# The S5 convolution kernel in four column groups, and its Toeplitz rows through DRAM

## The reference

```python
def s5_layer(u, lam_re, lam_im, log_dt, b_re, b_im, c_re, c_im, d_skip):
    ...
    bu_re = jnp.einsum('blgh,gph->blgp', uf, bb_re)
    bu_im = jnp.einsum('blgh,gph->blgp', uf, bb_im)
    ...
    _, _, xr, xi = lax.associative_scan(combine, (a_re, a_im, bu_re, bu_im), axis=1)
    y = (jnp.einsum('blgp,ghp->blgh', xr, c_re.astype(f32))
         - jnp.einsum('blgp,ghp->blgh', xi, c_im.astype(f32))
         + d_skip.astype(f32) * uf)
```

## Time and profile before

| | |
|---|---|
| time, median of 3 runs (least to most) | 980.72 us (980.63 to 980.98) |
| the profiled execution: its time / its span | 982.18 us / 980.4 us |
| TensorE busy | 895.5 us (91%) |
| VectorE / ScalarE / GpSimd busy | 303.9 / 179.2 / 168.0 us |
| moved by DMA | 254.32 MB, 259 GB/s on average |
| mean granted TensorE clock | 0.987 of full speed |

### The profile page before, as it was taken

The page is one execution under the profiler, slowest core; times in us unless marked ns, Lnnn a source line. Parts: engine busy times, 40 slices in busy tenths (PEclk is TensorE's granted clock), DMA queues, the critical chain, the costliest instruction groups (busy, mean ns, idle before and its releaser), DMA issues.

```text
span 980.4 us, 14278 instructions
## 1 busy us (share of the span) xinstructions
PE 895.5 (91%) x4978; PEld 508.5 (52%) x4978; DVE 303.9 (31%) x810; ACT 179.2 (18%) x403; POOL 168.0 (17%) x264
## 2 busy tenths in 40 slices
PE   8999999999999999999978898889888988887884
PEld 3445876554444444445845555555555555554432
DVE  4990675770111111125651111111111111111125
ACT  1222148661000000101111111111111111111121
POOL 2010013440000000000002222222222222222212
PEclk9999999999999999999989999999999999999978
DMA  8342844028322222091589999999999999999963
GB/s 311 72 82 98 100 46 162 2 76 369 136 75 75 76 75 76 10 380 44 204 350 422 417 420 421 422 420 421 421 422 420 423 422 421 425 420 425 423 250 145
DMA packets 44266, 254.32 MB, mean 259 GB/s; under 512 B 15103, under 2 KB 15631, under 8 KB 27812
## 3 DMA queue, kind: packets, MB, share of 16 engines
q1 hardware_dynamic: 33702, 243.38, 62.8%
q0 software_dynamic: 10240, 9.64, 3.8%
q10 hardware_dynamic: 288, 0.81, 0.2%
HBM read 256.28 MB, written 21.04 MB: 283 GB/s over the span
## 4 chain that ended last, share of the span: by engine, by line
PE 77%; SPq 8%; DMA 4%; DVE 4%; issue 3%; ACT 1%; POOLq 0%; POOL 0%; DVEq 0%; ACTq 0%
PE ps L671 20%; PE ps L810 16%; PE ps L830 9%; PE ps L449 6%; PE ps L707 6%; DMA reg_bo<-experts 4%; SPq L348 4%; SPq L355 3%; PE ps L441 3%; PE ps L797 2%; PE ps L628 2%; PE ps L584 2%; PE ps L606 2%; PE ps L510 2%; PE ps L820 1%
## 5 line engine op out<-in xcount | busy, mean ns | idle before, releaser
L810 PE MATMUL ps<-arena,reg_a 128*64 128x256 f32 x1024 | 117.8, 381 | 4.9 <-DMA arena<-experts 3.0
L1568 DVE TENSOR_TENSOR small<-reg_u,ps 128x128 f32<-128x128 f32 x62 | 17.9, 288 | 333.7 <-ACT reg_u L1067 333.7
L671 PE MATMUL ps<-xT,arena 128*128 128x512 f32 x256 | 111.2, 592 | 0.0
L810 PEld LDWEIGHTS ps<-arena,reg_a 128*64 128x64 f32 x1024 | 86.8, 138 | 43.7 <-issue 21.8
L1711 POOL DMA_INDIRECT ye_scratch<-reg_bo,reg_u x62 | 62.7, 1011 | 223.9 <-ACT reg_bo L1074 221.5
L671 PEld LDWEIGHTS ps<-xT,arena 128*128 128x128 f32 x256 | 48.6, 190 | 61.2 <-issue 61.2
L830 PE MATMUL ps<-arena,small 128*64 128x512 f32 x256 | 63.7, 616 | 13.9 <-issue 9.9
L1074 ACT COPY reg_bo<-ps 128x512 f32<-128x512 f32 x62 | 36.3, 585 | 208.8 <-PE ps L830 205.5
L671 PE MATMUL ps<-reg_u,arena 128*128 128x512 f32 x128 | 57.5, 592 | 0.0
L707 PE MATMUL ps<-reg_a,reg_bo 128*128 128x512 f32 x128 | 55.8, 593 | 0.0
L449 PE MATMUL ps<-xT,reg_bo 128*128 128x512 f32 x128 | 55.7, 594 | 0.0
(11 more groups left out here) (287 smaller groups left out, 1189.3 us busy)
## 6 DMA issues: line engine op xcount, KB each, us to landing
arena<-experts SPq DMA_DIRECT2D x32, 2048.0 KB
arena<-experts SPq DMA_DIRECT2D x32, 1024.0 KB
reg_bo<-experts SPq DMA_DIRECT2D x8, 2048.0 KB
reg_a<-experts SPq DMA_DIRECT2D x8, 2048.0 KB
arena<-mid_w SPq DMA_DIRECT2D x8, 1792.0 KB, 7.4
xT<-experts SPq DMA_DIRECT2D x7, 2048.0 KB
x<-experts SPq DMA_DIRECT2D x7, 2048.0 KB
reg_bo<-experts SPq DMA_DIRECT2D x8, 1024.0 KB
```

What stands on the lines that cost most here:

```text
L671: m = pe.matmul(ps[bank][:, :], w[:, (o + c) * P:(o + c + 1) * P], rhs[:, c, :], start=(c == 0), stop=(c == nk - 1))
L810: m = pe.matmul(ps[2 + c % 2][64 * h:64 * h + 64, 0:DE], xgT[:, x, BLK * (c % 2):BLK * (c % 2 + 1)], gates[k][:, x * 512 + h * DE:x * 512 ...
```

## The change

The products that make the convolution kernel are placed otherwise. Pair g = 4b + q now goes to the 32 rows of column group q and to 128 columns at block b of a single bank; the loops run b, then real and imaginary part, then q, so that consecutive products go to different column groups. One copy of 128 rows by 512 columns takes the whole bank to `kst`. The constants of the skip term (`s5d`, `eyeh`) are laid out for 128 rows, and VectorE's product of the two no longer waits for the copies.

The matrix `kst` is then written to DRAM (`kst_scratch`, 256 KB) in one transfer, counted by the new semaphore `s_kd`. The Toeplitz rows are read from there: eight transfers, one for each k, with 512 pieces each, of the same lengths as before. Five are issued by SP after the bias transfers, three by ScalarE ahead of the v copies; both wait for `s_kd`. TensorE waits once for the copy ahead of the v projection where it waited for one bank each time, and for 8 Toeplitz transfers instead of 16.

```diff
@@ -95,6 +95,7 @@
         SKEW, SKEW_C = 16, 8
         shift_dram = nc.dram_tensor("shift_scratch", (SKEW, HEADS, WB), F32, kind="Internal").ap()
         shift_c_dram = nc.dram_tensor("shift_c_scratch", (SKEW_C, HEADS, 2 * L), F32, kind="Internal").ap()
+        kst_dram = nc.dram_tensor("kst_scratch", (P, 4 * P), F32, kind="Internal").ap()
         x1_dram = nc.dram_tensor("x1_scratch", (L, D), F32, kind="Internal").ap()
         ye_dram = nc.dram_tensor("ye_scratch", (2 * 2 * L, D // 2), F32, kind="Internal").ap()
 
@@ -107,8 +108,8 @@
         b2row = sm.take(HD)
         post = sm.take(2 * SP2).rearrange("p (i m) -> p i m", i=2)
         posb = sm.take(2 * 2 * SP2).rearrange("p (i g m) -> p i g m", i=2, g=2)
-        s5d = sm.take(GP, 32)
-        eyeh = sm.take(SH, 32)
+        s5d = sm.take(4)
+        eyeh = sm.take(SH)
         rtbl = sm.take(HEADS, 33)
 
 
@@ -151,7 +152,7 @@
         apow = s5r.take(2 * GP * 9).rearrange("p (i g j) -> p i g j", i=2, g=GP)
         sp = [s5r.take(GP) for _ in range(40)]
         w1t = x1[:, :].rearrange("p (i g n) -> p i g n", i=2, g=GP)
-        kst = x1[0:32, 0:2048].rearrange("p (g n) -> p g n", g=GP)
+        kst = x1[:, 0:512].rearrange("p (b n) -> p b n", b=4)
         xs = x1[:, 2048:4096].rearrange("p (i g c) -> p i g c", i=2, g=GP)
         onehot = work[0:33, 0:2048]
         rsb = w1l.rearrange("p g n -> p (g n)")[0:HEADS, 0:2048]
@@ -293,6 +294,10 @@
         DONE = (2, 4, 8)
         NW = 2 * PAIRS
 
+        def toeplitz_rows(eng, k):
+            eng.dma_start(toep[SH * k:SH * (k + 1), :, (T8 - 1 - k) * SH:P].rearrange("p (b r) n -> p b r n", b=4),
+                          kst_dram.rearrange("(r h) (b n) -> h b r n", r=8, b=4)[:, :, :, 0:(k + 1) * SH]).then_inc(s_toep, 16)
+
         block = ctx.enter_context(nc.Block())
 
         R_K, R_W1, NRING = 2, 8, 12
@@ -325,17 +330,17 @@
                                           [[HEADS * 2 * L - CS, n], [4 * 2 * L, 2], [1, L]])).then_inc(s_be, 16)
 
             sp_.wait_ge(s_w1t, 1)
-            sp_.wait_ge(s_kmm, 4)
+            sp_.wait_ge(s_kmm, 1)
+            sp_.wait_ge(s_kst, 2)
+            sp_.wait_ge(s_zero, 4)
+            sp_.dma_start(kst_dram, x1[:, 0:512]).then_inc(s_kd, 16)
             for i in range(P // SKEW):
                 sp_.dma_start(biasT[SKEW * i:SKEW * (i + 1)],
                               bass.AP(shift_dram.tensor, P - 1 - SKEW * i, [[HEADS * WB - 1, SKEW], [WB, HEADS], [1, L]])).then_inc(s_bt, 16)
 
-            sp_.wait_ge(s_kst, 5)
-            sp_.wait_ge(s_zero, 4)
-            for k in range(T8):
-                for g2 in range(2):
-                    sp_.dma_start(toep[SH * k:SH * (k + 1), g2:SG:2, (T8 - 1 - k) * SH:P],
-                                  kst[SH * g2:SH * (g2 + 1), :, 0:(k + 1) * SH]).then_inc(s_toep, 16)
+            sp_.wait_ge(s_kd, 16)
+            for k in (7, 5, 4, 2, 0):
+                toeplitz_rows(sp_, k)
 
             sp_.wait_ge(s_y, 4)
             sp_.dma_start(mid[0], a["mid_w"][0]).then_inc(s_mid[0], 16)
@@ -487,12 +492,13 @@
             pe.wait_ge(s_ca, 1)
             pe.wait_ge(s_bbz, 1)
             pe.wait_ge(s_ublk, 4)
-            for g in range(GP):
-                out = ps[g // 4][0:32, (g % 4) * P:(g % 4 + 1) * P]
-                pe.matmul(out, bbz[:, 0, g, :], ca_re[:, g, 0:8, :], start=True, stop=False)
-                m = pe.matmul(out, bbz[:, 1, g, :], ca_ni[:, g, 0:8, :], start=False, stop=True)
-                if g % 4 == 3:
-                    m.then_inc(s_kmm, 1)
+            for b in range(4):
+                for ri in range(2):
+                    for q in range(4):
+                        g = 4 * b + q
+                        m = pe.matmul(ps[0][32 * q:32 * q + 32, b * P:(b + 1) * P], bbz[:, ri, g, :], (ca_re, ca_ni)[ri][:, g, 0:8, :],
+                                      start=(b == 0 and ri == 0), stop=(ri == 1), skip_group_check=True)
+            m.then_inc(s_kmm, 1)
 
             pe.wait_ge(s_w1l, 8)
             for g in range(GP):
@@ -504,8 +510,8 @@
             m.then_inc(s_s, 1)
 
             pe.wait_ge(s_wv, 16)
+            pe.wait_ge(s_kst, 1)
             for t in range(TT):
-                pe.wait_ge(s_kst, t + 1)
                 for c in range(KC):
                     m = pe.matmul(ps[t][:, 0:VC], xTc[:, c, t * P:(t + 1) * P], w_v[:, c, :],
                                   start=(c == 0), stop=(c == KC - 1))
@@ -640,7 +646,7 @@
             scores(0, 0)
             scores(0, 1)
             pe.wait_ge(s_xz, 1)
-            pe.wait_ge(s_toep, 16 * 16)
+            pe.wait_ge(s_toep, 16 * T8)
             pe.wait_ge(s_bce, 2)
             ssm_out(0)
             ssm_out(1)
@@ -941,9 +947,12 @@
                 if n == 0:
                     act.wait_ge(s_rd, 32)
                 act.copy(w1l[:, 4 * n:4 * n + 4, :], ps[4 + n % 4][:, :].rearrange("p (q n) -> p q n", q=4)).then_inc(s_w1l, 1)
-            for n in range(4):
-                act.wait_ge(s_kmm, n + 1)
-                act.copy(kst[:, 4 * n:4 * n + 4, :], ps[n][0:32, :].rearrange("p (q n) -> p q n", q=4)).then_inc(s_kst, 1)
+            act.wait_ge(s_kmm, 1)
+            act.copy(kst, ps[0][:, :].rearrange("p (b n) -> p b n", b=4)).then_inc(s_kst, 1)
+            act.wait_ge(s_zero, 4)
+            act.wait_ge(s_kd, 16)
+            for k in (6, 3, 1):
+                toeplitz_rows(act, k)
             for t in range(TT):
                 act.wait_ge(s_v, t + 1)
                 act.copy(vg[:, t, :], ps[t][:, 0:VC]).then_inc(s_vev, 1)
@@ -1261,11 +1270,11 @@
             u_blocks()
             w_matrices()
 
-            dve.wait_ge(s_kst, 4)
-            sk = work[0:32, 0:256].rearrange("p (g h) -> p g h", g=GP)
-            link(tt(sk, s5d.unsqueeze(2).broadcast_to([32, GP, SH]), eyeh.unsqueeze(1).broadcast_to([32, GP, SH]), ALU.mult))
+            sk = work[:, 0:4 * SH].rearrange("p (b h) -> p b h", b=4)
+            link(tt(sk, s5d.unsqueeze(2).broadcast_to([P, 4, SH]), eyeh.unsqueeze(1).broadcast_to([P, 4, SH]), ALU.mult))
+            dve.wait_ge(s_kst, 1)
             dve.tensor_tensor(kst[:, :, 0:SH], kst[:, :, 0:SH], sk, ALU.add).then_inc(s_kst, 1)
-            dve.wait_ge(s_kst, 5)
+            dve.wait_ge(s_kst, 2)
 
             dve.wait_ge(s_s, 1)
             half = lambda t, i: t[:, 512 * i:512 * (i + 1)].rearrange("p (g c) -> p g c", g=8)
@@ -1785,7 +1794,7 @@
     cm = lambda n: pair(f(n)[0]).transpose(1, 3, 0, 2).reshape(P, GP * SH)
     s5 = np.concatenate([lam("s5_lambda_re"), lam("s5_lambda_im"), dt, bm("s5_b_re"), bm("s5_b_im"),
                          cm("s5_c_re"), cm("s5_c_im")], 1)
-    s5d = pair(f("s5_d")[0]).transpose(1, 2, 0).reshape(32, GP)
+    s5d = pair(f("s5_d")[0]).reshape(4, 4, 2, SH).transpose(1, 2, 3, 0).reshape(P, 4)
 
     dist = np.arange(-L, L)
     n = np.maximum(dist, 0)
@@ -1803,7 +1812,7 @@
     gu = gu.transpose(0, 2, 1, 3, 4, 5).reshape(NE, P, KC * 2 * DE)
     dn = wd.reshape(NE, 2, P, D).transpose(0, 2, 1, 3).reshape(NE, P, 2 * D)
     experts = np.concatenate([gu, dn], 2).reshape(NE * P, EW)
-    eyeh = np.tile(np.eye(SH, dtype=np.float32), (2, 1))
+    eyeh = np.tile(np.eye(SH, dtype=np.float32), (8, 1))
     router = part(np.concatenate([f("router_w_group")[0], f("router_w_expert")[0]], 1))
     ix = np.arange
     rc = np.zeros((P, NRC), np.float32)
```

More of the change, by code:

```diff
@@ L263, in build_kernel @@
         s_toep = sem("s_toep"); s_s = sem("s_s"); s_sev = sem("s_sev"); s_xz = sem("s_xz")
-        s_y = sem("s_y"); s_yev = sem("s_yev"); s_ytp = sem("s_ytp"); s_z = sem("s_z")
+        s_kd = sem("s_kd"); s_y = sem("s_y"); s_yev = sem("s_yev"); s_ytp = sem("s_ytp"); s_z = sem("s_z")
         s_v = sem("s_v"); s_vb = sem("s_vb"); s_vev = sem("s_vev")
```

## The result

| | before | after |
|---|---|---|
| time, median of ten runs each on one chip (least to most) | 980.58 us (980.08 to 980.98) | 974.1 us (973.03 to 978.2) |
| the profiled execution: its time / its span | 982.18 / 980.4 us | 973.58 / 971.8 us |
| TensorE busy | 895.5 us | 885.0 us |
| mean granted clock | 0.987 | 0.992 |

The ratio over all ten runs is 0.9943 with an interval of [0.9933, 0.9952]: 0.6% faster, 6.5 us between the medians. The ten runs of the kernel after scatter over 5 us, those before over 1 us, so the same kernel was run again later (experiment 10): 976.23 us, ratio 0.9959 [0.9945, 0.9973], inside the range. The median of all fifteen runs is 975.8 us.

What follows compares the result with a forecast made beforehand. TensorE's chain in the front part, then the DMA-full expert weight stream from 500 us, bound the kernel. One term, -5.1 us, takes the profiled 982.18 to 977.1; the timed median, 1.5 lower, gives 975.7 us, range 974.6 to 979.3.

Steps and rivals of the forecast that it cites:

- The products: 32 convolution kernel products on TensorE's chain: four column groups cut 7.1 to 2.0 us, 5.1 less (3.2 to 5.3).
- What waits behind them: Work after the kernel products: its waits stay satisfied, 1 us left instead of 6 for the L943 copies; no cost.
- ScalarE's queue: ScalarE waits for the DRAM write (by 106) and issues three transfers, ending at 110 to 118.4; no cost.
- The transfers: DRAM write and Toeplitz reads end at 131.6, needed at 135.1: cost 0, up to 9.5 us at the upper end.
- the old pace: Toeplitz pieces out of DRAM move as those out of SBUF did, 13 us at 99 GB/s.
- The bias transfers: Issued 3.5 us earlier, sharing DMA engines with ScalarE's transfers; land by 122, wanted by the minima at 139.8.
- No loss on the way: After the front part: TensorE's unbroken stretch begins at 217.5 instead of 222.6.
- The last stage: Expert weight stream, DMA full from 500 us: TensorE's gain moves its start and end by the same amount.
- pairing of groups by two: Rival for the kernel products: column groups overlap only two at a time, gain 3.2, 977.5 us; chance 0.09.
- a wait moved to the landing: Rival at the Toeplitz landing or ScalarE's issues: part is lost, gain 1 to 4, about 978.5 us; chance 0.07.
- small pieces at double cost: Rival at the Toeplitz reads: pieces out of DRAM cost double, landing at 144.6; loses 4.4 us, 985.1 us; chance 0.07.
- a loss later: Rival: the gain is lost later, in the DMA-full stretch from 500 us, or groups do not overlap; 980.7 us; chance 0.05.

Runs made afterwards that it cites:

- experiment 10: The kernel after the change, run again with no edit: 976.23 us, ratio 0.9959 to the kernel before.
- Experiment 3: The kernel after the change, with 24 idle products (5.2 us together) put ahead of the 32 kernel products: 979.86 us, ratio 0.9997.
- experiment 5: The kernel after the change, with the loop over column groups outermost, 16 records in a row to one group: 977.91 us, ratio 0.9978.
- experiment 9: The kernel after the change, with real and imaginary product of a pair in a row, then the next group: 974.79 us, ratio 0.9938.
- experiment 6: The kernel after the change, with all Toeplitz transfers on SP, each cut into four by columns (16384 pieces): 985.37 us, ratio 1.0046.
- experiment 7: The kernel after the change, with 12 idle products in TensorE's wait before the experts: 973.53 us, ratio 0.9927.
- experiment 8: The kernel before the change, with 12 idle products in TensorE's wait before the experts: 979.43 us, ratio 0.9989.
- experiment 11: The kernel after the change, with all Toeplitz transfers on SP and 12 idle products in the wait before the experts: 974.27 us, ratio 0.9934.
- experiment 1: The kernel after the change, but Toeplitz rows straight from SBUF in 64 transfers on SP, no DRAM write: 988.53 us, ratio 1.0083.

## Why the prediction was right, step by step

- **The products** (7.1 to 2.0 us, 5.1 saved): 1.88 us, 5.23 saved in the profile. It lies between the two ways of getting the 2.0, by streaming in four groups (1.78) and by the pace of the records of L501 (1.94); the factor is 7.11 / 1.88 = 3.8. Experiment 3 shows it to be the cause of the time, experiments 5 and 9 that it comes from overlap between groups. The figure of the Trainium skill (TensorE: Matmul & The Clock Gate, its table of measured speedups by packing) of 2.38 times for three column tiles did not bound this case: four groups reached 3.8 of 4.
- **What waits behind them**: nothing, as said, the margin to the `w1l` copies being 0.9 us where I had 1. That the former four copies cost nothing holds. VectorE's addition took 0.23 us under my bound of 0.41.
- **ScalarE's queue**: released earlier than my bound, since the write landed in 2.0 us, not 5.8, and done with its issues at 103.9 against 110 to 118. My mark for the first v copy, 107 to 112, was too late: it ran at 105.4, or 106.7 with the 1.3 us by which this execution was early. It waits for its product, and the issues end before.
- **The transfers**: forecast to end at 131.6 against a need at 135.1. By the profile they end by 128 against a need at 133.65; put on the scale of the profile before, 1.3 us later, 129.3 against 134.95. The spare time is 5.7 us, not 3.5, since small pieces out of DRAM moved at 113 GB/s where those out of SBUF had 99, and part of them moved earlier, beside the bias rows. I had chosen the old pace; the lower bound of 128 was nearer. The Trainium skill (DMA: Bandwidth & Descriptors, "Why small descriptors are slow (HBM only)") puts the penalty for small pieces on HBM and frees SBUF to SBUF of it. Here, at 64 to 512 bytes, no such difference is to be seen. For pieces of 16 to 128 bytes experiment 6 doesn't settle it.
- **The bias transfers**: no cost, as said; VectorE's chain ends in the minima at 138.42 (139.7 on the scale of before, forecast 139.8).
- **No loss on the way**: TensorE's unbroken stretch starts at 216.05 (217.35 on the scale of before, forecast 217.5), and the router's products still have the 6.53 us.
- **The last stage** is the one step that was right in its result and wrong in part of its reason. I wrote that the stream of weights passes a microsecond on because TensorE's products release its fetches. The 421 GB/s of every profile from 550 to 800 us say that the stream is limited by the DMA engines; a gain ahead of it is kept because the stream starts earlier, as I also wrote, and of what TensorE loses at its start only a part is left at the last expert: 1.3 of 4.5 us in experiment 10. For the clock I had no term. The sum had 977.1 us for the profiled execution, and it took 973.58. Of the 3.5 us, 1.3 lie ahead of the change, 0.1 in the block, 0.6 between the router and the last expert, and 1.4 behind the last expert, where the kernel before had its clock at 1.2 GHz for about 10 us and this execution for about 7. The execution profiled of before took 1.6 us more than its kernel's median (982.18 us against 980.58).
- **What was luck.** The term of the block was right to 0.1 us, and for the reason given. That the medians of the two sets, 974.1 and 976.23, lie on either side of 975.7 and within 1.6 us of it is partly luck: the start of the program, the drop and the stage behind the experts each moved an execution by about 1 us or more, and the sum had none of them.

The rivals: pairing of groups by two falls with 1.88 us; a wait moved to the landing falls with the rows of L536; small pieces at double cost fell; a landing made late in another way (experiment 6) cost about as much as it was late, as the working had it; a loss later fell with the table above.

Left open: why the clock drops in some executions of the change after the same wait and in others not, what sets the length of the drops, and what sets the 1.3 us at the start of the program. Experiments 7, 8 and 11 took the drop at the experts away by an edit; the stretch behind the last expert and the start of the program are only seen in the traces.

## What to carry to other kernels

Small products on the critical path that fill a quarter of the columns of the array are worth placing in four column groups, in an order that changes the group at least every few records: here 3.8 times faster, and hardly at all if the groups come one after another. Count what the new layout does to the transfers behind it before building it: here SP took 0.6 us or more for each issue, so the same gain turned into a loss with 64 transfers and held with eight, at the price of a round trip through DRAM. And where a later stage is full with DMA, ask when it fills: the gain ahead of it was kept whole here, while 4.5 us lost by TensorE as it filled came down to 1.3.

## What the runs showed of the hardware that I had not expected

- Products in different column groups overlap nearly in full with four records of one group in a row (1.96 us for the block) and hardly with 16 (5.89 us). Lengths between were not run.
- A wait of 10 to 13 us of TensorE costs more than itself: the first S5 outputs behind it took 3.68 us where they take 1.96, and the clock was at 1.2 GHz from 136.5 to 153.5 in experiment 1 and from 135.3 to 149.0 in experiment 6, and after the wait of 2.75 us before the experts it was at 1.2 GHz for about 10 us in one execution and not in another. Twelve idle products in that wait kept it at 2.4 GHz in each of the three profiles taken with them.
- The pace of the first projection differs between executions of the same program: between 7.2 and 9.7 us the kernel before has 8 matmul records and the one after 14, and the whole block takes 30.36 us in the one and 29.21 in the other (29.8 to 30.7 in the others where the view shows it whole). The column of the granted clock has 1.00 in both. The window of the kernel before:

```profile
7.20:9.70 2.50, 2.50 (x8) 0.68 (x6) 0.93 (x6) 0.21 (x1) 1.22 (x3) 1.00 1.09 269
```

and of the one after:

```profile
7.20:9.70 2.50, 2.50 (x14) 1.09 (x12) 1.60 (x9) 0.22 (x1) 1.26 (x3) 1.00 1.04 260
```

- A transfer of 256 KB from 128 partitions to DRAM landed in 2.0 us, where one of 512 KB took 5.8 in the kernel before.
